# Ring slots shared unevenly, a pipelined linear attention and five more adaLN units on VectorE in a two-layer diffusion step

## The reference, cut to what matters

```python
mod = silu(cond) @ w_ada + b_ada                 # 12 blocks of 512 columns: "ada units" 0 to 11
h = rmsnorm(x) * (1 + sc1) + sh1
q, k, v, gq, gk, gv, gg, lr_f, lr_b, ga, gb = split(h @ w_in)
o_attn = softmax attention (8 heads, 2 kv heads; latent tokens also see 128 cached keys)
o_gla  = bidirectional gated linear attention (4 heads), gated rmsnorm
x = x + g1 * ((sigmoid(ga) * (o_attn @ w_pa) + sigmoid(gb) * (o_gla @ w_pb)) @ w_out)
x = x + g2 * grouped_moe(rmsnorm(x) * (1 + sc2) + sh2)      # 16 experts, top 2 of the best group
```

## Time and profile before

| | us |
|---|---|
| median of 3 runs | 1016.63 |
| the three runs | 1022.54, 1016.63, 1014.25 |
| the profiled execution's own time | 1020.26 |
| its span, first to last instruction | 1018.1 |
| TensorE busy | 961.9 (94%) |
| VectorE busy | 383.7 (38%) |
| ScalarE busy | 237.6 (23%) |
| GpSimd busy | 99.9 (10%) |

### The profile page before, as it was taken

One profiled execution on the slowest core, in us unless ns is written; L12 is line 12 of the kernel. 1 busy time (PEld: TensorE's weight loads), 2 busy tenths in 40 slices (PEclk: granted clock), 3 DMA queues, 4 the chain that ended last, 5 costly groups with the idle time before them and its releaser, 6 DMA issues.

```text
span 1018.1 us, 13639 instructions
## 1 busy us (share of the span) xinstructions
PE 961.9 (94%) x4894; PEld 564.6 (55%) x4894; DVE 383.7 (38%) x1011; ACT 237.6 (23%) x521; POOL 99.9 (10%) x85
## 2 busy tenths in 40 slices
PE   6999999999989999999899999899899999999987
PEld 2348877777845443443344687777686444344333
DVE  4098612783261222222351421258535222222124
ACT  2113222521123222121140322352101232122111
POOL 0000003741100000000000000066310000000000
PEclk8999999999999999999999999999999999999999
DMA  9899552246989998999998533240877999989992
GB/s 392 372 364 420 209 203 102 109 192 269 416 346 411 418 422 361 423 421 421 426 427 352 194 110 139 83 166 6 336 296 284 402 407 423 421 365 421 421 421 100
DMA packets 37378, 317.48 MB, mean 312 GB/s; under 512 B 4280, under 2 KB 4432, under 8 KB 5328
## 3 DMA queue, kind: packets, MB, share of 16 engines
q1 hardware_dynamic: 36144, 311.28, 74.8%
q0 software_dynamic: 1184, 5.53, 1.4%
HBM read 314.93 MB, written 1.86 MB: 311 GB/s over the span
## 4 chain that ended last, share of the span: by engine, by line
PE 77%; DMA 13%; DVE 5%; ACT 3%; issue 2%; SPq 0%; ACTq 0%; DVEq 0%
PE ps L1015 18%; DMA ring<-w_gu 12%; PE ps L563 11%; PE ps L1027 7%; PE ps L709 7%; PE ps L904 5%; PE ps L973 3%; PE ps L890 3%; PE ps L727 3%; PE ps L822 2%; PE ps L576 2%; PE ps L667 2%; PE ps L543 1%; PE ps L988 1%; PE ps L676 1%
## 5 line engine op out<-in xcount | busy, mean ns | idle before, releaser
L1015 PE MATMUL ps<-ring,tmq 128*64 128x512 f32 x928 | 212.4, 598 | 18.3 <-DMA ring<-w_gu 14.8
L1015 PEld LDWEIGHTS ps<-ring,tmq 128*64 128x64 f32 x928 | 67.8, 138 | 143.5 <-issue 126.4
L563 PE MATMUL ps<-more,ring 128*128 128x256 f32 x512 | 114.3, 381 | 0.5 <-ACT more L1084 0.5
L1027 PE MATMUL ps<-ring,tmq 128*64 128x512 f32 x512 | 113.8, 596 | 0.0
L563 PEld LDWEIGHTS ps<-more,ring 128*128 128x128 f32 x512 | 96.1, 190 | 15.5 <-issue 2.5
L1848 DVE TENSOR_TENSOR tmq<-tmq,ps 128x256 f32<-128x256 f32 x32 | 13.5, 421 | 206.0 <-ACT tmq L1339 206.0
L1084 ACT ACTIVATE tmq<-ps 128x256 f32<-128x256 f32 (+3 forms) x124 | 55.6, 462 | 149.2 <-PE ps L709 62.8
L1027 PEld LDWEIGHTS ps<-ring,tmq 128*64 128x64 f32 x512 | 35.2, 137 | 65.7 <-issue 62.1
L709 PE MATMUL ps<-ring,more 128*128 128x512 f32 (+1 forms) x192 | 69.9, 523 | 0.0
L1859 DVE SCALAR_TENSOR_TENSOR x<-ps,mod,x 128x128 f32<-128x128 f32 x256 | 67.6, 342 | 1.9 <-PE ps L973 1.9
L1339 ACT ACTIVATE tmq<-ps 128x256 f32<-128x256 f32 x32 | 12.3, 383 | 226.1 <-PE ps L1015 226.1
(11 more groups left out here) (254 smaller groups left out, 1031.1 us busy)
## 6 DMA issues: line engine op xcount, KB each, us to landing
ring<-w_gu SPq DMA_DIRECT2D x116, 1024.0 KB, 14.3
ring<-w_down SPq DMA_DIRECT2D x64, 1024.0 KB, 12.5
ring<-w_ada SPq DMA_DIRECT2D x24, 2048.0 KB, 11.3
ring<-w_in SPq DMA_DIRECT2D x14, 2048.0 KB, 17.4
ring<-w_out SPq DMA_DIRECT2D x4, 2048.0 KB, 10.8
more<-w_gu SPq DMA_DIRECT2D x8, 1024.0 KB, 14.6
cst<-consts SPq DMA_DIRECT2D x2, 2080.0 KB, 16.0
ring<-w_in SPq DMA_DIRECT2D x4, 1024.0 KB, 23.3
```

The source lines that it names most:

```text
L563: mm = pe.matmul(ps[:, 5, i * NT:(i + 1) * NT], w[:, k, m * P:(m + 1) * P], h[:, k, :], start=k == 0, stop=k == KT - 1)
L1015: mm = pe.matmul(ps[r:r + SLOTS, half, :].rearrange("p (j n) -> p j n", j=2), hg[:, k, e, 0:SLOTS], gu_unit(l, kh, e, in_more)[:, part, :, ...
L1027: mm = pe.matmul(ps[r:r + SLOTS, 2 + n, :], at_[:, k, r:r + SLOTS], down_unit(l, k // 2)[:, e, k % 2, n * 512:(n + 1) * 512], start=k == 0 ...
```

## The change

- The last dense units of each layer (from (l, "pa", 0) on) go round only four of the six ring buffers (`NARROW`). The other two (`AHEAD`) take the units 0 and 1 of expert pair 0, loaded once the gate and ada units that were there are used, ahead of the out units. Slots, turns and predecessors are now tables (`place_units`: `SLOT`, `TURN`, `PRIOR`, `EXPERT_SLOT`) in place of n % RING.
- VectorE computes ada units 4 to 8 of layer 0 and 6 to 9 of layer 1: nine units instead of four. The remaining ada fills of layer 0 (9, 10, 11) stand ahead of gate chunks 4, 5 and 6, in the attention stage. The layer 1 list has none.
- VectorE's `ada_blocks` are also run in layer 1, and the one block after the first softmax becomes (1, 4, 0, 0) over the four softmaxes. `cs_rows` is loaded in both layers, ahead of the other layer parameters; the state comes after the last ada unit of VectorE in both.
- pa is done in eight halves of four products (`pa_half`), one in each head, in place of four chunks.
- GLA is pipelined by one head: `gla_out(i - 1)` and `gla_keys(i - 1)` run in iteration i, around `gla_levels(i)`. Levels alternate between banks 2, 3 and 6, 7. VectorE makes `qe(i + 1)` before it masks head i, and `kst` moves from GpSimd to VectorE. `qin` gets a second buffer. The rmsnorm of the first half is cut in two steps over two iterations.
- At the start, `WARM` goes from 6 to 10 dummy matmuls, and `keep_busy(2)` puts two dummy matmuls at two places among the first ada units.

```diff
-VECTOR_ADA = (4, 5, 6, 7)
+VECTOR_ADA = [(4, 5, 6, 7, 8), (6, 7, 8, 9)]
...
 def fill_list(l):
...
+    gates = [[("gate", c)] for c in range(8)]
     if l + 1 < LAYERS:
...
+        for c, a in zip(range(4, 7), range(VECTOR_ADA[l][-1] + 1, ADA)):
+            gates[c].insert(0, ("ada", a))
+    halves = [[("pa", i)] for i in range(8)]
+    return gates + [slot for half in halves for slot in (half, HOLE)]
...
-WARM = 6
+WARM = 10
...
+AHEAD = 2
+NARROW = RING - AHEAD
...
+def place_units():
+
+    slot, turn, prior, expert_slot = [], [], [], []
+    last, loads = [None] * RING, [0] * RING
+    cycle = list(range(RING))
+    for l in range(LAYERS):
+        units = layer_units(l)
+        wide = units.index((l, "pa", 0))
+        for j in range(len(units)):
+            at = cycle[(j if j < wide else wide + (j - wide) % NARROW) % RING]
+            slot.append(at)
+            prior.append(last[at])
+            turn.append(loads[at] + 1)
+            last[at], loads[at] = len(slot) - 1, loads[at] + 1
+        ahead = [cycle[(wide + NARROW + i) % RING] for i in range(AHEAD)]
+        cycle = ahead + slot[-NARROW:]
+        expert_slot.append(cycle)
+    return slot, turn, prior, expert_slot
...
             def ada_a(l, a):
 
                 w = full(l, "ada", a)
-                if l == 0 and a == VECTOR_ADA[-1] + 1:
-                    pe.wait_ge(ada_mod, a)
+                if a == VECTOR_ADA[l][-1] + 1:
+                    pe.wait_ge(ada_mod, ada_turn(l, a))
...
+            def keep_busy(n):
+
+                for _ in range(n):
+                    pe.matmul(ps[:, 3, :], x[:, 0, 0:P], x[:, 0:2, :].rearrange("p k n -> p (k n)"), start=True, stop=True)
...
                     ada_a(l, FIRST_ADA[1])
+                    keep_busy(2)
                     ada_b(l, FIRST_ADA[1])
+                    keep_busy(2)
                     first_half(0)
...
                     pe.wait_ge(g_ke, n + 1)
-                    if i:
-                        pe.wait_ge(g_st, n)
+                    if i == 1:
+                        pe.wait_ge(ada_mod, fills_done(l))
+                    if i >= 2:
+                        pe.wait_ge(g_st, n - 1)
...
                     if i < 7:
                         gla_in(i + 1)
+                    if 0 < i <= GH:
+                        gla_keys(i - 1)
                     gla_levels(i)
-                    if i < GH:
-                        gla_keys(i)
+                    if i:
+                        gla_out(i - 1)
                     fill(l)
-                    gla_out(i)
+                gla_out(7)
...
                     act.wait_ge(g_dec, n + 1)
                     if i >= 2:
-                        act.wait_ge(g_qe, n - 1)
                         act.wait_ge(g_ke, n - 1)
-                        act.wait_ge(g_kst, 4 * l + min(i - 1, GH))
+                        act.wait_ge(g_st, n - 1)
...
-                        if 2 * s + v == 0:
-                            ada_blocks(l, 1)
+                        ada_blocks(l, (1, 4, 0, 0)[2 * s + v])
...
                 for i in range(8):
                     fill(l)
-                    gla_mask(i)
                     if i < 7:
                         gla_q(i + 1)
+                    gla_mask(i)
+                    if i + 1 < GH:
+                        gla_kst(i + 1)
                     fill(l)
```

More of the change, by code:

```diff
@@ L10 @@
 from contextlib import ExitStack
+import itertools
 import numpy as np
@@ L116, in on_vector @@
 def on_vector(l, a):
-    return l == 0 and a in VECTOR_ADA
+    return a in VECTOR_ADA[l]
 def tensor_turn(l, a):
     turn = ada_turn(l, a)
-    return turn - sum(ada_turn(0, i) < turn for i in VECTOR_ADA)
+    return turn - sum(ada_turn(ll, i) < turn for ll in range(LAYERS) for i in VECTOR_ADA[ll])
 POOL_LOADS = [["cs_out", "cs_rows", "lparams", "state", "shift_out", "shift_rows"],
-              ["lparams", "shift_out", "shift_rows"]]
+              ["cs_rows", "lparams", "state", "shift_out", "shift_rows"]]
 def loaded(l, name):
@@ L173, with fills_done, level_bank @@
 EARLY = 1
-WARM = 6
+WARM = 10
+def fills_done(l):
+    return ADA * l + max([VECTOR_ADA[l][-1]] + [n for slot in fill_list(l) for kind, n in slot if kind == "ada"]) + 1
+def level_bank(i):
+    return 6 if i % 2 else 2
 def gain_turn(l, n):
     return 2 * l + n + 2
[L182 to L202, removed]
@@ new lines, in layer_units @@
+def layer_units(l):
+    out = [] if l else [(0, "ada", a) for a in FIRST_ADA[:2]] + HALVED + [(0, "ada", a) for a in FIRST_ADA[2:]]
+    out += [(l, "ada", a) for a in early_units(l)]
+    vector = [(l, "ada", a) for a in VECTOR_ADA[l]]
+    for n in range(len(IN_UNITS)):
+        if (l, "in", n) not in HALVED:
+            out.append((l, "in", n))
+        if n in (1, 3 if l else 2):
+            out.append(vector.pop(0))
+    for kind, n in itertools.chain(*fill_list(l)):
+        if kind == "ada" or (kind, n) == ("pa", 0):
+            out.append((l, kind, n))
+        elif kind == "gate" and n % 2 == 0:
+            out.append((l, "gates", n // 2))
+            for _ in range((1, len(vector))[n // 2] if n < 4 else 0):
+                out.append(vector.pop(0))
+    out += [(ll, "ada", a) for ll, a in front(l)[:1]] + [(l, "pb", 0)] + [(ll, "ada", a) for ll, a in front(l)[1:]]
+    out += [(l, "out", 0), (l, "out", 1)] + [(ll, "ada", a) for ll, a in tail(l)]
@@ L203, in dense_order @@
     return out
-ORDER = dense_order()
+ORDER = [key for l in range(LAYERS) for key in layer_units(l)]
 PLACE = {key: n for n, key in enumerate(ORDER)}
 HALVES_IN = 16 * len(HALVED)
-BEFORE = [max(PLACE[(l, "out", 1)], *(PLACE[(ll, "ada", a)] for ll, a in window(l))) + 1 for l in range(LAYERS)]
+AHEAD = 2
[17 more added lines that the diff above has]
+    return slot, turn, prior, expert_slot
@@ L213, in build @@
+SLOT, TURN, PRIOR, EXPERT_SLOT = place_units()
+FIRST = [sum(len(layer_units(ll)) for ll in range(l)) for l in range(LAYERS + 1)]
+AHEAD_AT = [PLACE[(l, "pa", 0)] + NARROW for l in range(LAYERS)]
 def build(nc, xT, consts, params, lparams, w_ada, w_in, w_pa, w_pb, w_out, w_gu, w_down,
@@ L472, in _ @@
             for l in range(LAYERS):
-                while n < BEFORE[l]:
-                    if n >= RING:
-                        sp.wait_ge(*used(n - RING))
+                while n < FIRST[l + 1]:
+                    if n == AHEAD_AT[l]:
+                        for u in range(AHEAD):
+                            first_expert(l, u)
+                    if PRIOR[n] is not None:
+                        sp.wait_ge(*used(PRIOR[n]))
                     if ORDER[n] == (l, "gates", 0):
@@ L590, in fill @@
                 flush()
-                if fills:
-                    kind, n = fills.pop(0)
+                for kind, n in fills.pop(0) if fills else []:
                     if kind == "ada":
@@ L1905, in _ @@
             for l in range(LAYERS):
-                late = 0 if l else GH * DV
+                late = GH * DV
                 if l:
```

178 lines of the change are left out of this document (96 added, 82 removed).

## The result

| | before | after |
|---|---|---|
| median (range) | 1017.4 us (1014.25 to 1022.54, 4 runs) | 1028.51 us (1026.82 to 1031.3, 4 runs) |
| ratio to before | | 1.0107 [1.0075, 1.0138] |
| profiled execution, span | 1020.26, 1018.1 | 1027.59, 1025.8 |
| TensorE / VectorE / ScalarE / GpSimd busy | 961.9 / 383.7 / 237.6 / 99.9 | 959.7 / 441.0 / 233.9 / 103.7 |

A forecast was written before the change was run, and what follows sets the result against it. TensorE was taken to bound the kernel outside the experts, loads within them. Terms -3.0 + 7.7 + 4.2 - 5.6 - 5.6 = -2.3 us, carried to the median, gave 1014.3 us; range 1002 to 1027.

The forecast's parts named there:

- The sum: Whole kernel: start, three moved units, the wait for unit 8 and GLA in both layers add up to -2.3 us.
- GLA, -5.6 a layer: GLA, gate 7 to last out: 54.9 us becomes 49.3, with waits at heads 1, 3 and 7 included.
- behind the sigmoids: GLA, head 1: `gla_out(0)` waits about 1.8 us for the key copy, which ScalarE does after the gate sigmoids.
- The wait for unit 8, +4.2: Attention, layer 0: TensorE waits 4.2 us at ada 9 until VectorE has finished ada unit 8.
- three units moved, +7.7: Layer 0: three ada units move from GLA to attention at 2.55 us each, +7.7 there.
- The tail behind the last out: End of GLA: norm, scaling and turn are the same chain on other engines and keep their length.
- The start, -3.0: Kernel start: extra dummies and `keep_busy` hold the clock, so the first input products save 3.0 us (bounds 0 to 3.3).
- Ring and early experts 0: Loads before the experts: the queue has already caught up with the buffers, so the expert stages keep their length, 0.
- VectorE's blocks 0: Layer 1: VectorE's new ada blocks fall in its gaps and cost nothing.
- The median: Step from profiled execution to median: before's median 1016.63 lies 3.6 us below its profile, taken over to give 1014.3.
- the clock: Rival: dummies don't hold the clock at the start and GLA's longer pauses drop it; +8.5 us, 1025.1, chance 0.14.
- GpSimd wins the meeting: Rival, GLA: `ke` starts before `qe` in each head, stage 56.4 us, +1.5 a layer; 1028.5, chance 0.13.

The follow-up runs named there:

- experiment 3: The changed kernel with the `qin` product moved behind mask and reduction to `st`; median 1020.49 us, ratio to before 1.0026.
- experiment 4: The changed kernel with exp(i+2) waiting for the readers of its buffer instead of `st(i)`; span 1017.5 us.
- Experiment 10: The kernel before, old GLA order, with the four ada units of each GLA stage moved behind gate chunks 3 to 6 in attention; span 1042.2 us.
- experiment 1: The changed kernel with the ada units of layer 0 behind their gate chunks instead of ahead; median 1021.27 us, ratio to before 1.0032.
- experiment 2: The changed kernel with five dummy products ahead of ada 9's wait and the `ada_copied` wait moved ahead of them; attention of layer 0 87.7 us, against 89.9.
- experiment 5: The changed kernel with three dummy products at GLA's end, one behind the last out and two between the turns of the halves; span 1022.5 us.
- experiment 11: The changed kernel itself, profiled once more with nothing changed; span 1023.7 us.
- experiment 7: The changed kernel with the start of before (`WARM` 6, no `keep_busy`); first gate chunk at 94.2 us, against 93.9.
- experiment 9: The kernel before with only the new start (`WARM` 10, `keep_busy` twice); median 1017.3 us, ratio to before 0.9992.
- experiment 6: The changed kernel with no expert units ahead (`AHEAD` 0), late dense units round all six ring buffers; median 1026.93 us, ratio to before 1.0064.

## Why the prediction was wrong

The sum said -2.3 for the profiled execution; +7.7 was measured.

- *GLA, -5.6 a layer.* Measured -3.1 and -3.2; by the forecast's measure, from the end of gate 7 on, 51.7 and not 49.3. The step that failed: "One loop is therefore qe 1.1, mask and reduction 2.7, exp 1.0, and then qe and ke in turn, 3.2: 8.0 us and a levels step, for two heads of 11.4 on TensorE." The rows of 211.40 to 218.22 show the loop go round once for one head, since `qe(i+1)` stands ahead of mask(i) on VectorE and exp(i+1) waits for st(i-1); and the turn-taking with `ke` falls between `qe` and `qin`, so that it lies inside the loop. One turn is 1.0 + 2.1 + 1.3 + 1.3 + 1.1 = 6.8, against TensorE's 5.6. From the order of instructions in the diff this could be read. Experiments 3 and 4 opened the loop and gained 2.3 and 2.5. The sum was too low by 2.5 and 2.4. That the loop is worth just what was missed is in part luck. Counted by rows, TensorE waited 6.7 (5.3 forecast): 1.44 behind the sigmoids (1.8 forecast), 1.59 at head 7 as forecast, nothing at head 3 (1.5 to 2 forecast), and the rest at the loop, at `st` of the last heads and 0.32 put down to "issue". Its own rows took 45.0, a microsecond more than the forecast's 44.7 less 0.7, 0.8 of it because eight halves of pa, 1.83 from start to start, stand for four chunks of 3.45. Experiment 10 shows the same failure from the other side: with four ada units of 10.2 taken out, the old order gets only 1.2 shorter at full clock, since waits come up in their place.
- *The wait for unit 8, +4.2, and three units moved, +7.7.* The wait measured 3.98; its mechanism and its size were right. The three units cost 7.1 (experiment 1). The term of the wait was mis-sized by what it left out: the clock behind the pause, 2.3 in this profile (experiment 2). Attention took 89.9 where 88 was written.
- *"The tail behind the last out ... keeps its length".* The step failed in the profiled execution, by 2.8 with pb in layer 0 and 0.8 in layer 1, again through the clock (experiments 5 and 11). In layer 0 it is not shown to be the change's doing: the second profile of the same kernel has the tail at 6.4, below the 6.6 of before.
- *The start, -3.0.* -3.1 in the two profiles, with the rows as forecast, but the 3.0 was no fixed cost of the kernel before (experiments 7, 9 and 10).
- *Ring and early experts 0, VectorE's blocks 0.* Right: experiment 6, and layer 1's stages of 74.6 and 76.0 without a change, though VectorE's busy time in the latter rose from 13.7 to 30.8 us:

```profile
602.40:678.50 76.10, 71.69 (x392) 60.03 (x391) 30.80 (x48) 18.22 (x52) 7.68 (x4) 1.00 0.43 170
```

- *The median.* It was made by taking off 3.6 us, by three runs of before with a median of 1016.63. Medians of 17 to 19 runs of before lie at 1018.6 to 1019.5, some 2.4 higher. Of the 14.2 us that were missed, 9.6 are the sum's (-2.3 against the +7.3 from 1020.26 to 1027.59). The rest is the step to the median: 3.6 were taken off, while the changed kernel's median lies 0.9 above its profiled execution.

Of the rivals, the clock had a part of the cause but the wrong places: it foresaw falls in GLA and a lost start, and the falls came behind the pause in attention and at GLA's end. "GpSimd wins the meeting" gave nearly the measured time, 1028.5, for a reason that does not hold: VectorE went first in seven of eight heads of layer 0, and GLA took 51.7, not 56.4.

What stays open is why the clock falls in one execution and not in another with the same rows. And whether the three ada units would be cheaper back in GLA's heads 4 to 7, where TensorE has 1.2 us to spare in each head, wasn't tried.

## What to carry to other kernels

Before a stage is pipelined to save an engine's waits, ask what fills these waits now: the four ada units of layer 0 cost 1.2 us in the old order, and the three that moved cost 7.1 where they went. Lay a software loop out per iteration and in the order in which each queue issues, and put every wait for a buffer into it: the longest ring counts, and an instruction that nobody needs yet (`qin`) belongs behind those that somebody waits for. Price a new pause of TensorE at its length plus the slower products behind it, and fill a pause that can't go.

## What was not expected of the hardware

- With GpSimd waiting at the port, VectorE's next instruction lost its turn although its row begins as `qe`'s ends: 2.17 us for a `qin` of 0.28, six times in a run.
- Behind a pause of 1.62 us the clock fell to 0.50 in one execution and not in another of the same kernel (238.65 and 237.54 above). Behind the pause of 3.98 us it fell in all eight profiles that have it. A fall cost 0.5 to 3 us, in the experts 1.4 to 1.7 behind waits for loads. The spread of before's runs, 1014 to 1026 us, goes with it: its granted clock is 0.997 in a run of 1013.99 and 0.985 in one of 1024.29. The Trainium skill, "TensorE: Matmul & The Clock Gate", Part 1, says that the number of slow products at a kernel's start varies between runs of one kernel; the trace agrees for the start, where the first ada product took 3.61, 3.58 and 1.92 us in three profiles of kernels with the same start, and shows the same in the middle of a kernel.
